# Norms over 1024 columns: a ScalarE square root and a VectorE reciprocal in place of a logarithm and an exponential

## What is computed

```
y = xc * lax.rsqrt(var + eps) * g + b            # LayerNorm (_layernorm), over 1024 columns, twice
y = x * lax.rsqrt(mean(x * x) + eps) * g         # RMS norm before and after FFN 1, mixer, FFN 2: six times
h = rms_norm(x, ffn1_pre_g[l])
x = x + 0.5 * rms_norm(swiglu(h, ffn1_w_in[l], ffn1_w_out[l]), ffn1_post_g[l])
...
mixed = jnp.concatenate([attn, ssm], axis=-1) @ w_mix_out[l]
x = x + rms_norm(mixed, mix_post_g[l])
```

## Time and profile before

| | |
|---|---|
| median of 3 executions | 3384.59 us (3380.22 to 3388.14) |
| profiled execution, its own time | 3386.24 us |
| its span | 3384.6 us |
| mean clock granted to PE | 0.982 |
| busy | PE 95%, DVE 61%, ACT 38%, POOL 11% |

### The profile page before, as it was taken

How to read it: one execution, slowest core, us unless ns; L and a number is a source line. 1 busy time by engine, 2 the same in 40 slices (tenths; PEclk the granted TensorE clock), 3 DMA queues, 4 the chain that set the end, 5 groups by cost and what they waited for, 6 DMA issues and landing times.

```text
span 3384.6 us, 39667 instructions
## 1 busy us (share of the span) xinstructions
PE 3217.2 (95%) x15804; PEld 2532.4 (75%) x15804; DVE 2065.0 (61%) x2774; ACT 1294.8 (38%) x1907; POOL 377.3 (11%) x405
## 2 busy tenths in 40 slices
PE   8998999999999998899999999998889899999998
PEld 6765676878777786578888877785667778888877
DVE  5555566664555646777776656676564877766334
ACT  2564434442525343643233224314434442323123
POOL 1000000110302011200000003140011300000012
PEclk9999999999999999899999999999989999999999
DMA  6210111222423122332224243322244332225232
GB/s 155 49 41 5 54 51 52 78 82 75 100 51 107 56 90 71 101 106 88 75 88 161 97 134 106 112 60 85 25 99 137 115 114 83 75 100 168 80 114 100
DMA packets 363254, 299.39 MB, mean 88 GB/s; under 512 B 55104, under 2 KB 324896, under 8 KB 362784
## 3 DMA queue, kind: packets, MB, share of 16 engines
q1 hardware_dynamic: 340800, 215.17, 22.3%
q0 software_dynamic: 22272, 81.69, 7.4%
HBM read 240.32 MB, written 52.95 MB: 87 GB/s over the span
## 4 chain that ended last, share of the span: by engine, by line
PE 73%; DVE 12%; DMA 5%; ACT 5%; issue 4%; SPq 1%; POOL 0%; ACTq 0%; DVEq 0%; POOLq 0%
PE PS L364 41%; PE PS L2450 12%; PE PA L2450 7%; DMA CDX<-ssd_decays 3%; PE PS L864 2%; DVE WL L328 1%; DVE CDX L1999 1%; PE PA L875 1%; PE PB L1778 1%; DVE XL L2127 1%; DMA WS<-in_ffn_w_out_dram 1%; PE PB L887 1%; PE PA L404 1%; PE PB L1781 1%; DVE ACC L2104 1%
## 5 line engine op out<-in xcount | busy, mean ns | idle before, releaser
L364 PE MATMUL PS<-XH,WH 128*128 128x512 f32 x1744 | 603.2, 405 | 36.6 <-DVE XL L2127 19.7
L364 PE MATMUL PS<-XL,WH 128*128 128x512 f32 x1744 | 579.6, 391 | 0.0
L364 PE MATMUL PS<-XH,WL 128*128 128x512 f32 x1744 | 579.1, 391 | 0.0
L321 ACT ACTIVATE WH<-WS 128x1024 fp32r<-128x1024 f32 (+1 forms) x243 | 240.4, 993 | 846.6 <-PE PS L364 793.7
L364 PEld LDWEIGHTS PS<-XH,WH 128*128 128x128 f32 x1744 | 326.5, 189 | 136.2 <-DVE XL L2127 27.6
L364 PEld LDWEIGHTS PS<-XH,WL 128*128 128x128 f32 x1744 | 328.7, 188 | 69.9
L364 PEld LDWEIGHTS PS<-XL,WH 128*128 128x128 f32 x1744 | 328.7, 188 | 69.3 <-issue 1.8
L328 DVE TENSOR_TENSOR WL<-WS,WH 128x1024 fp32r<-128x1024 f32 (+1 forms) x243 | 284.2, 1170 | 142.7 <-ACT WH L321 142.4
L364 PE MATMUL PS<-TQH,WH 128*128 128x512 f32 x448 | 161.4, 395 | 7.0 <-DVE WL L328 7.0
L364 PE MATMUL PS<-TQL,WH 128*128 128x512 f32 x448 | 160.2, 392 | 0.0
L364 PE MATMUL PS<-TQH,WL 128*128 128x512 f32 x448 | 160.1, 392 | 0.0
(11 more groups left out here) (683 smaller groups left out, 6169.9 us busy)
## 6 DMA issues: line engine op xcount, KB each, us to landing
RAW<-in_ffn_w_in_dram SPq DMA_DIRECT2D x36, 1024.0 KB, 5.3
WS<-in_ffn_w_out_dram SPq DMA_DIRECT2D x48, 512.0 KB, 3.7
WS<-in_ssd_w_in_dram SPq DMA_DIRECT2D x40, 512.0 KB, 3.8
DEC<-ssd_decay_sums SPq DMA_DIRECT2D x32, 512.0 KB, 3.8
WS<-in_ffn_w_in_dram SPq DMA_DIRECT2D x32, 512.0 KB, 4.0
CDX<-ssd_decays SPq DMA_DIRECT2D x56, 256.0 KB, 4.7
TQF<-ffn_hidden POOLq DMA_DIRECT2D x14, 1024.0 KB, 8.0
x_residual<-ACC POOLq DMA_DIRECT2D x6, 2048.0 KB, 7.7
```

Source lines behind the costliest of these rows:

```text
L321: nc.scalar.activation(WH[:, s, 0:cols], WS[:, s, 0:cols], ACT.Copy).then_inc(W_HI[s], 1)
L364: last = nc.tensor.matmul(PS[s][0:width, c], w[:, s, k * width:(k + 1) * width], x[:, k, c], start=(k == 0 and j == 0), stop=(k == kt - 1 ...
```

## The change

The factor is now made in two steps on two engines. ACT takes the square root of the sum (mean plus eps) and signals; DVE takes the reciprocal of that tile in place, as a new instruction in its own queue just ahead of the first multiplication by it, and waits for its own write. Fifteen tiles of 128x512 are made so (four in the LayerNorms, six before and five after a stage), and the four columns at the end. Norms over fewer columns (`norm_rstd`, line 390) keep Ln and Exp. Two small activations that ran Ln on one column ahead of time run Sqrt, and LN 2 gets one too. For their own semaphore the reciprocals use two of the old `XLD` semaphores, which stand at 16 since the start. PE's few waits on `RSTD` and `P_RSTD` now let it go at the square root.

```diff
-    def ln_rstd(act, st, name, h):
+    def ln_root(act, name, h):
         c = half(h)
         act.wait_ge(SUMMED, NORM[name][1] + KT * (h + 1))
-        st.link(nc.scalar.activation(T[0][:, c], PA[:, c], ACT.Ln, bias=EP[:, EPS5:EPS5 + 1], scale=1.0 / D))
-        nc.scalar.activation(T[1][:, c], T[0][:, c], ACT.Exp, scale=-0.5).then_inc(RSTD, 1)
+        nc.scalar.activation(T[1][:, c], PA[:, c], ACT.Sqrt, bias=EP[:, EPS5:EPS5 + 1], scale=1.0 / D).then_inc(RSTD, 1)
+
+    def ln_inverse(dve, st, name, h):
+        dve.wait_ge(RSTD, NORM[name][0] + h + 1)
+        st.link(nc.vector.reciprocal(T[1][:, half(h)], T[1][:, half(h)]))
...
     def ln_scalar(act, st, turn, name, b):
+        nc.scalar.activation(EP[:, 14:15], EP[:, 0:1], ACT.Sqrt)
         for k in range(KT):
...
         for h in range(2):
             c = half(h)
-            dve.wait_ge(RSTD, NORM[name][0] + h + 1)
+            ln_inverse(dve, st, name, h)
...
+    def post_inverse(dve, u, h):
+        n = 2 * (u - 1) + h + 1
+        dve.wait_ge(P_RSTD, n)
+        nc.vector.reciprocal(RPS[u][:, h], RPS[u][:, h]).then_inc(P_INV, 1)
+        dve.wait_ge(P_INV, XLD_END + n)
 
     def post_apply(dve, u, h, rows):
         if rows and rows[0] == 0:
-            dve.wait_ge(P_RSTD, 2 * (u - 1) + h + 1)
+            post_inverse(dve, u, h)
...
-    def between_rstd(act, st, u):
-
-        post_log(act, st, u, 1)
-        pre_log(act, st, u, 0)
-        pre_exp(act, u, 0)
-        post_exp(act, u, 1)
+    def between_roots(act, u):
+
+        post_root(act, u, 1)
+        pre_root(act, u, 0)
...
     def mix_vector(dve, st):
         tt = nc.vector.tensor_tensor
         for h in range(2):
-            dve.wait_ge(Q_RSTD, 2 + h + 1)
+            pre_inverse(dve, 1, h)
...
     def out_vector(dve):
         dve.wait_ge(P_RSTD, 6)
+        nc.vector.reciprocal(SM[:, 4:8], SM[:, 4:8]).then_inc(P_INV, 1)
+        dve.wait_ge(P_INV, XLD_END + 6)
```

More of the change, by code:

```diff
@@ L481, in _build @@
     XLD = [sem(f"x_tile_loaded{s}") for s in range(TT)]
+    XLD_END = 16
     XTURNED, XHI, XCOP = sem("x_tile_turned"), sem("x_tile_hi"), sem("x_tile_copied")
@@ L1346, in out1_vector @@
                     for k in LN1_APPLY.get(m, ()):
-                        ln1_apply(dve, 0, k)
+                        ln1_apply(dve, st, 0, k)
                     for k in LN1_LOW.get(m, ()):
@@ L1352, in out1_vector @@
             if k < KT:
-                ln1_apply(dve, 1, k)
+                ln1_apply(dve, st, 1, k)
             if k >= 2:
@@ L1375, in out1_scalar @@
                         ln1_square(act, 0, k)
-                    nc.scalar.activation(EP[:, 12:13], EP[:, 0:1], ACT.Ln)
+                    nc.scalar.activation(EP[:, 12:13], EP[:, 0:1], ACT.Sqrt)
                 if m == 1:
-                    ln_rstd(act, st, "ln1", 0)
+                    ln_root(act, "ln1", 0)
                 for k in LN1_HIGH.get(m, ()):
@@ L1382, in out1_scalar @@
             ln1_square(act, 1, k)
-        nc.scalar.activation(EP[:, 13:14], EP[:, 0:1], ACT.Ln)
-        ln_rstd(act, st, "ln1", 1)
+        nc.scalar.activation(EP[:, 13:14], EP[:, 0:1], ACT.Sqrt)
+        ln_root(act, "ln1", 1)
         for k in range(KT):
@@ L1461, in ln_scalar @@
             if k == 5:
-                ln_rstd(act, st, name, 0)
+                ln_root(act, name, 0)
             ln_square(act, turn, 1, k)
@@ L1465, in ln_scalar @@
             if h == 1:
-                pre_rstd(act, st, 0, 0)
+                pre_root(act, 0, 0)
             for k in range(KT):
                 if h == 0 and k == 5:
-                    ln_rstd(act, st, name, 1)
+                    ln_root(act, name, 1)
                 ln_bias(act, turn, b, h, k, LNB)
@@ L2084, in post_rows, with post_root @@
         nc.tensor.matmul(PA[:, half(h)], ONES[:], RPS[u][:, h], start=True, stop=True).then_inc(P_ROWS, 1)
-    def post_log(act, st, u, h):
+    def post_root(act, u, h):
         act.wait_ge(P_ROWS, 2 * (u - 1) + h + 1)
[L2088 to L2095, removed]
+        nc.scalar.activation(RPS[u][:, h], PA[:, half(h)], ACT.Sqrt, bias=EP[:, EPS6:EPS6 + 1], scale=1.0 / D).then_inc(P_RSTD, 1)
+    def post_inverse(dve, u, h):
[3 more added lines that the diff above has]
+        dve.wait_ge(P_INV, XLD_END + n)
     def post_apply(dve, u, h, rows):
         if rows and rows[0] == 0:
-            dve.wait_ge(P_RSTD, 2 * (u - 1) + h + 1)
+            post_inverse(dve, u, h)
             if h == 0:
@@ L2139, in pre_rows, with pre_root, pre_inverse @@
         nc.tensor.matmul(PB[:, half(h)], ONES[:], RPRE[:, half(h)], start=True, stop=True).then_inc(Q_ROWS, 1)
-    def pre_log(act, st, u, h):
+    def pre_root(act, u, h):
         act.wait_ge(Q_ROWS, 2 * u + h + 1)
[L2143 to L2152, removed]
-    def between_rstd(act, st, u):
-        post_log(act, st, u, 1)
-        pre_log(act, st, u, 0)
-        pre_exp(act, u, 0)
-        post_exp(act, u, 1)
+        nc.scalar.activation(RPRE[:, half(h)], PB[:, half(h)], ACT.Sqrt, bias=EP[:, EPS6:EPS6 + 1], scale=1.0 / D).then_inc(Q_RSTD, 1)
+    def pre_inverse(dve, u, h):
+        n = 2 * u + h + 1
+        dve.wait_ge(Q_RSTD, n)
+        nc.vector.reciprocal(RPRE[:, half(h)], RPRE[:, half(h)]).then_inc(Q_INV, 1)
+        dve.wait_ge(Q_INV, XLD_END + n)
+    def between_roots(act, u):
+        post_root(act, u, 1)
+        pre_root(act, u, 0)
     def tail_tensor(pe, u, hi, lo, kt, ready):
@@ L2196, in tail_scalar @@
                     if m == 0:
-                        post_rstd(act, st, u, 0)
+                        post_root(act, u, 0)
                     for k in TAIL_HIGH.get(m, ()) if u < 3 else ():
@@ L2205, in tail_scalar @@
         if u == 2:
-            between_rstd(act, st, u)
+            between_roots(act, u)
     def tail_pool(pool, u):
@@ L2239, in head_scalar @@
         if j == 6:
-            pre_rstd(act, st, u, 1)
+            pre_root(act, u, 1)
     def head_pool(pool, u):
@@ L2740, in ffn_vector @@
         for h in range(2):
-            dve.wait_ge(Q_RSTD, 2 * u + h + 1)
+            pre_inverse(dve, u, h)
             for f in range(FFN_HEAD):
@@ L3441, in out_scalar @@
         act.wait_ge(P_ROWS, 6)
-        st.link(nc.scalar.activation(SM[:, 0:4], PA[:, 0:4], ACT.Ln, bias=EP[:, EPS6:EPS6 + 1], scale=1.0 / D))
-        nc.scalar.activation(SM[:, 4:8], SM[:, 0:4], ACT.Exp, scale=-0.5).then_inc(P_RSTD, 1)
+        nc.scalar.activation(SM[:, 4:8], PA[:, 0:4], ACT.Sqrt, bias=EP[:, EPS6:EPS6 + 1], scale=1.0 / D).then_inc(P_RSTD, 1)
     def out_sync(sp):
```

5 lines of the change are left out of this document (3 added, 2 removed).

## The result

The changed kernel takes 3394.11 us (median of 13 runs, 3383.51 to 3402.3), and the kernel before took 3384.3 (13 runs, 3380.22 to 3391.28) beside it. The ratio is 1.0021 with a 95% interval of 1.0013 to 1.003. A second set gave 3395.48 against 3386.03, ratio 1.003 (1.002 to 1.004). So the change costs 9.8 and 9.4 us by the medians, and by the ratios 7.1 us (4.4 to 10.2) and 10.2 us (6.8 to 13.5). The forecast was +5.1, that is 3389.7, with a range from 3385 to 3396. The sign was right, the time lies in the range, and the size was half to seven tenths of what was measured.

A forecast was written before the change was run, and what follows sets the result against it. PE was taken to hold most of the chain, so ACT and DVE changes count only where PE waits for them. The terms 1.35 - 4.2 + 4.4 + 2.4 + 0.2 + 1.0 = +5.1 us gave 3389.7, range 3385 to 3396.

The forecast's parts named there:

- Price of a reciprocal: On DVE, a reciprocal of 512 columns was taken to last 3.36 us, worked out from two smaller sizes.
- Rival (d): Slower, about 3397: a reciprocal costs eight DVE clocks a column, 1.05 us more a tile at seven exposed tiles; chance 0.05.
- Tails: Tails of FFN 1 and of the mixer: the exposed reciprocal, less a refund at the scalings, costs +2.2 each, +4.4 together.
- Mixer's head: Head of the mixer: +2.4 from the second post factor ahead of a scaling, and +0.2 at the factor of half 1.
- LN 1: Half 0's delay vanishes in DVE's idle time; half 1 moves DVE's queue by 1.45, some 0.1 of it hidden: +1.35.
- FFN 2's head: Head of FFN 2: the first read moves by 0.3, the post factor's 3.36 partly fills idle times: +1.0.
- Second factors and FFN 2's tail: Half 1 before FFN 1 and FFN 2, and the tail of FFN 2: DVE's idle time covers the delay, 0 each.
- LN 2: ACT's queue sets the pace there; with loads saved, PE restarts at 1415.0 to 1416.0, not before 1415.3: -4.2.
- PE's filler: In LN 2, PE's filler work of 6.64 us, which ended at 1418.54, would end at 1415.3.
- Rival (c): Slower, about 3393: LN 2 gives back only 1 us, since DVE takes over from ACT in setting the pace; chance 0.13.
- rival (b): Slower, 3392 to 3394: reciprocal and POOL collide in both tails, or PE falls to 1.2 GHz before FFN 2; chance 0.25.

## Why the prediction was right, and where it fell short

**Price of a reciprocal:** 3.35, right. Rival (d), eight clocks for a column, is out: 15 reciprocals ran at 3.34 to 3.35. An estimate from the repeat count of eight that the Trainium skill gives ("VectorE: DVE Perf Modes", "First, the fixed hardware budget") would be 4.3 us; the measurement decides.

**Tails:** 2.20 to 2.23 for 2.2, twice, in three kernels and four profiles. Shown, by the run with the tails alone, by the row of POOL beside the reciprocal and by the scalings at 1.41.

**Mixer's head:** 2.24 to 2.31 for 2.6. **LN 1:** 1.44 for 1.35 in the run where the clock did not interfere; half 0 came back to 0.01 after its scaling had come 1.4 late, as said. **FFN 2's head:** 0.8 for 1.0. **Second factors and FFN 2's tail:** nothing, as said (in the tail 0.26 was left at 3344.60 and gone by the next block), and the threefold reciprocal showed how much cover there was.

**LN 2** is the term that was mis-sized: -4.2 forecast, -3.35 and -2.51 in the two profiles of the changed kernel, -2.70 in the run with LN 2 alone, and -2.2 by its time. The prediction moved DVE's last low part by the whole 3.2 that ACT gained and said that DVE "can lose a little of it" by collisions with POOL. It lost half. The three last low parts, which before stood apart and waited for ACT (0.75 each), now run together in 4.10, where three of them alone take 2.25; POOL's additions (1.74 and 1.36 long, from 1399.82 and 1401.88) stand beside them. The rest of that paragraph came out within 0.4, but for PE's filler, which ended 0.6 earlier than said and decided nothing: the scalings without their collision (5.39 for 5.4), Silu straight after the read with its load hidden, PE 2.89 behind Silu. Even the -3.35 leans on one slow profile: the kernel before ran this stage in 88.08, and four other runs with old code there took 86.5 to 88.0. The mean of the five is 87.2, that of the three with new factors 85.2, a gain of 2.0 in place of 4.2. The run that added one reciprocal tells what the forecast didn't ask: the first factor was called free because DVE took it up late, and it is free only against the old factor. Against one call it costs 3.0 to 3.5. Rival (c), a gain of 1 only because DVE takes over from ACT, had the mechanism right, and the size lies between it and the forecast.

**The rest** is 1 to 4 us that no term held. The sum of the stages as the least disturbed profiles have them (for LN 2 the smaller of its two) is 1.44 - 2.5 + 4.4 + 2.3 + 0.8 = +6.4, and +7.1 and +10.2 were measured by the ratios (+9.8 and +9.4 by the medians). +6.4 lies in the first interval (4.4 to 10.2) and just under the second (6.8 to 13.5). If for each stage of the table the mean of all profiles with new code is set against the mean of all with old code, the sum is +7.5: LN 1 gives 0.8 and LN 2 -2.0 then, and FFN 2's head 2.0. The S5 stage isn't in it and would add 3.7, from four profiles and five. So the forecast was right in its sign and in most of its terms. That its total came out low is one mis-sized term, LN 2, and a remainder that isn't explained; that the measured time still lies in the range owes something to the range's width.

In the profile of the changed kernel four short drops of PE's clock (LN 1, FFN 1's head, and twice in FFN 2's head, together 6.3 us), which before's hadn't there, could hold the remainder. That is near rival (b)'s mechanism, but not where rival (b) put it: in both tails the granted clock stayed 1.00. Whether the change brings more drops isn't shown. In FFN 2's head the four profiles with new factors there had 2, 1, 3 and 2 drops, two of them without cost; of those with old ones before's had none and three others one each. In FFN 1's head, where old and new alike had none or one, and in LN 1 there is no such order. Eight profiles are too few to settle it. It stays open.

## What to carry to other kernels

Taking a load off one engine and putting a longer instruction on another is worth the saving only at the places where the first engine sets the pace; here that was one stage of seven, with three of the sixteen edits, and the other thirteen brought nothing or lost. Price each place by what stands right behind the new instruction in its queue, and treat an idle time as a cover: up to it the cost is zero. Beyond it the cost went one for one at two of the four places where it was tried; at the other two the cover was larger than the nearest idle times said. If a single function gives the value (here the reciprocal square root, whose accuracy must suffice), it beats both forms, and most of the gain (7.0 of 8.5 us) came from the three places where the wait is.

## What was unexpected in the hardware

Within one kernel the same stage repeats to 0.05 us where PE's clock holds, and jumps by 1.1 to 1.7 us when the clock falls to 1.2 GHz for a moment while PE's work is what the others wait for. A drop elsewhere can cost nothing: in FFN 2's head of the run that changed all but LN 2, DVE's next `WL` behind it stood 0.01 from before. Single profiles of one kernel thus differ by 8 us (spans 3395.9 and 3387.4 of the changed kernel), more than half of it in the S5 stage with its late transfer (4.7). Differences of a stage without drops can be read from single profiles at 0.1 us; differences of a span, or of a stage with a drop in one of the two, cannot.
